# Where a two-layer network computes its modulation vectors: two of them leave the first mixer, and the second norm is modulated per channel

## Chip, cores and metric

One Trainium2 chip, one core of it. The metric is the device time of one execution in microseconds (us); the kernel before takes 2913.27 us (median of 3 runs, 2911.15 to 2913.72).

## What is computed

Two layers over 256 context and 512 latent tokens of width 1024, in fp32. Each layer takes six modulation vectors for the context and six for the latent tokens from `silu(c) @ w_ada[l] + b_ada[l]`. A vector pair (context, latent) is named (l, r) here, r = 0 to 5: shift, scale and gate of the mixer, then of the mixture of experts.

```python
for l in range(2):
    mod = split(silu(c) @ w_ada[l] + b_ada[l], 6)        # once for c, once for c_ctx
    h = rmsnorm(x, g_mix[l]) * (1 + mod[1]) + mod[0]
    x = x + mod[2] * (mixer_ab(h) if l == 0 else mixer_c(h))   # conv + pooling; mLSTM
    h = rmsnorm(x, g_ffn[l]) * (1 + mod[4]) + mod[3]
    x = x + mod[5] * moe(h)                               # 16 experts, top 2
out = rmsnorm(x_lat, g_final)
```

## The kernel before

All engines run one program written out by hand; each engine executes its instructions in that order, and semaphores join them. Most of the program is matrix work on TensorE (PE).

The stages in order of time: the start (norm of the input, modulation vectors (0, 0) and (0, 1)); the first mixer (value, gate and pool products on PE, a 31-tap convolution on VectorE (DVE), a pooling chain on GpSimd (POOL), then a layernorm over channels, whose sums are PE products with `onesd`, and the output projection); routing, and a scatter of the tokens into expert order by GpSimd's indirect DMAs; experts(0), a loop of 18 passes; the gap between experts(0) and the second mixer, in which chain(2) gathers the experts' rows, adds them to x, norms them and turns them to channels; the second mixer (product with `w_in_c`, in which every operand is split in a high and a low part and three fp32r products replace one fp32 product; gates; values; keys and queries; 16 attention units); its projection, routing, scatter and experts(1); the last norm.

**Modulation work.** `w_ada` is read in items. Eight items of 256 columns ("units", `n < UNITS`) give (0, 2) and (0, 3). From `n = UNITS` on, four items of 1 MB give one vector of `VECTORS`. `mods(n)` on PE waits for the item's load, and multiplies it with `scT` (two columns). The first item of a vector also adds the bias (`bada`). After the fourth, `vector_out(w)` on ScalarE (ACT) takes the 2 x 1024 result out of PSUM, and stores it in DRAM (`mods_d`), from where a chain loads it spread over 128 partitions (`load_mods`). Each fp32 product is two rows' worth of `x` in the trace (a count of 8 is four products). The table `ITEMS_AT` says after which step of the first mixer how many items have been done; sixteen items, vectors 0 to 3, stand there, and the other sixteen in the gap.

**chain(n)** norms tile t of 128 tokens: ACT takes the sum of squares and the root, DVE scales (`normed`), PE turns the tile to channels (`to_channels`), ACT copies it out of PSUM (`turned`). There is one pair of PSUM banks for the turned tile, so that tile t + 1 waits for `turned` of tile t. In chain(2) DVE also takes the low part from PSUM (`low_input`), and PE waits for that too.

**Pooling on PE** (`pooled` 6 and 7) waits for the last pooling step of GpSimd, and PE, which runs in order, has work behind that wait.

Of the kernel before, what the change touches and what calls it, by code (L numbers as in the profile page):

```python
# [51 lines left out]
NPAR = TAPS + 6  # L52
# [60 lines left out]
def program(nc, x, c, ctx_in, c_ctx, w_ada, b_ada, g_mix, g_ffn, g_final, w_in_ab, w_dw_a, b_dw_a, ln_g_a, ln_b_a,  # L113
# [13 lines left out]
    with es:  # L127
# [131 lines left out]
        MOD_OF = {0: (None, None), 1: ((0, 3), (0, 2)), 2: ((1, 0), (0, 5)), 3: ((1, 3), (1, 2)), 4: (None, (1, 5))}  # L259
        G_OF = {0: g_mix[0], 1: g_ffn[0], 2: g_mix[1], 3: g_ffn[1], 4: g_final}  # L260
        MODS = []
        for n in range(5):
            per = (2 if MOD_OF[n][0] else 0) + (1 if MOD_OF[n][1] else 0)
            MODS.append(MODS[-1] + 16 * (1 + per * (1 if n >= 3 else 2)) if n else 0)
# [22 lines left out]
        chl = [rounded(f"chl{i}", o, 2, 2048) for i, (o, n) in enumerate(CHUNKS[1:4])]  # L287
# [9 lines left out]
        def item_at(n):  # L297

            if n < UNITS:
                return at(26624 + 2048 * (n % 2), KD, UW)  # L300
            return at(26624 + 2048 * ((n - UNITS) % 3) if n < I_GAP else 14336 + 2048 * ((n - I_GAP) % 8), 2, D)

        def vector_ps(w):

            b = (0 if w % 2 == 0 else 3) if w < W_GAP else 2 * (w % 2)
# [8 lines left out]
        hTh, hTl = rounded("hTh", 0, KD, S), rounded("hTl", 44144, KD, S)  # L314
        craw = nc.alloc_sbuf_tensor_at("craw", [P, KD, 512], F32, offset=base + 4 * 30832)[:]
# [38 lines left out]
        def _(sp):  # L354
# [20 lines left out]
            for r, v in enumerate((b_dw_a, ln_g_a, ln_b_a, b_pool.rearrange("a g d -> a (g d)"), pool_scale, g_mix[0:1, :])):  # L375
# [17 lines left out]
            def load_mods(n):  # L393
# [12 lines left out]
                sp.dma_start(CH[n]["tmp"], G_OF[n].partition_broadcast(P)).then_inc(s_mod, 16)  # L406
# [17 lines left out]
            def chain(n):  # L424
# [5 lines left out]
                for i, (t, j) in enumerate(tiles):  # L430
# [9 lines left out]
                    if n == 2 and i < 4:  # L440
                        for m in (I_GAP + 8 + 2 * i, I_GAP + 9 + 2 * i):
                            sp.wait_ge(u_mm, m - 7 if i < 3 else I_GAP + 10)
                            item_load(m)
# [47 lines left out]
            sp.wait_ge(a_mm, 7)  # L491
# [26 lines left out]
            for i in range(2):  # L518
                sp.wait_ge(u_st[i], stored(W_GAP))
# [7 lines left out]
            for n in range(I_GAP, I_GAP + 8):  # L527
# [1493 lines left out]
```

## Time and profile before

| | |
|---|---|
| median of 3 runs | 2913.27 us |
| profiled execution, its own time | 2915.74 us |
| its span, first to last instruction | 2914.1 us |
| mean granted TensorE clock | 0.948 of 2.4 GHz |
| PE busy | 2665.9 us, 91% |
| DVE busy | 1838.9 us, 63% |
| ACT busy | 1295.8 us, 44% |
| POOL busy | 311.6 us, 11% |
| DMA | 675.38 MB, mean 232 GB/s |

The busy share is a mean over all stages. What an edit is worth is read at its place: which engine the others wait for there.

### The profile page before, as it was taken

What the parts mean: (1) busy time and instruction counts of PE and PEld (TensorE: products, weight loads), DVE (VectorE), ACT (ScalarE), POOL (GpSimd) and SP (SyncE); (2) the same over time, 40 slices, a digit from 0 to 9 for tenths busy, and PEclk for the clock granted to TensorE, in tenths of its full rate; (3) what the DMA queues carried; (4) which work ended last, traced back from release to release, by engine and by line L of the source; (5) the groups of instructions that cost most, each with busy time, mean ns of one, the idle gap of its engine ahead of it and who ended that gap; (6) DMA issues with size and microseconds to landing.
All of it is one profiled execution on the core that took longest, in us unless ns stands there. A gap on an engine that the chain in (4) does not pass through costs nothing.

```text
span 2914.1 us, 29092 instructions
## 1 busy us (share of the span) xinstructions
PE 2665.9 (91%) x10607; PEld 1839.7 (63%) x10607; DVE 1838.9 (63%) x1678; ACT 1295.8 (44%) x1201; POOL 311.6 (11%) x299
## 2 busy tenths in 40 slices
PE   8999989992999999999899997899795899999994
PEld 3555424452888888888268775555343788888883
DVE  4899813124888888888557312355322788888886
ACT  4000002012777777777221321355210677777773
POOL 0537540002000000000200020000001000000001
PEclk9999999995999999999999978999896899999997
DMA  8021174518999999997921311001406799999993
GB/s 305 29 72 56 34 269 181 197 70 326 372 388 385 391 388 384 382 389 297 374 76 58 114 36 55 0 26 37 159 36 260 300 383 387 385 386 389 385 380 129
DMA packets 157055, 675.38 MB, mean 232 GB/s; under 512 B 24745, under 2 KB 42233, under 8 KB 100544
## 3 DMA queue, kind: packets, MB, share of 16 engines
q1 hardware_dynamic: 134416, 595.27, 53.2%
q0 software_dynamic: 20208, 74.98, 6.8%
q10 hardware_dynamic: 2368, 4.28, 0.4%
q8 instruction: 41, 0.67, 0.1%
q14 instruction: 22, 0.18, 0.0%
HBM read 615.13 MB, written 59.35 MB: 231 GB/s over the span
## 4 chain that ended last, share of the span: by engine, by line
PE 87%; DMA 5%; DVE 4%; POOL 2%; ACT 2%; issue 1%; SPq 0%; POOLq 0%; DVEq 0%; ACTq 0%
PE ps L723 83%; PE ps L881 1%; ACT arena L1157 1%; PE ps L887 1%; DMA arena<-in_w_ada_dram 1%; DMA buf_d<-arena,slots 1%; POOL buf_d L650 1%; DMA arena<-buf_d,slots 1%; POOL arena L611 1%; DMA xs_d<-arena 0%; DMA chunk<-in_w_ada_dram 0%; PE ps L825 0%; DMA arena<-in_w_out_c_dram 0%; PE ps L1052 0%; DMA buf_d<-arena 0%
## 5 line engine op out<-in xcount | busy, mean ns | idle before, releaser
L1693 DVE TENSOR_TENSOR wl<-wx,wh 128x2048 fp32r<-128x2048 f32 x432 | 969.4, 2286 | 45.5 <-ACT wh L1157 45.5
L1157 ACT ACTIVATE wh<-wx 128x2048 fp32r<-128x2048 f32 x432 | 819.5, 1915 | 185.8 <-PE ps L723 147.6
L723 PE MATMUL ps<-arena 128*128 128x512 f32 (+3 forms) x2432 | 853.6, 511 | 47.8 <-DVE arena L1836 20.1
L723 PE MATMUL ps<-wh,xT 128*128 128x512 f32 x2304 | 736.7, 396 | 4.9 <-DVE xT L1710 4.9
L723 PEld LDWEIGHTS ps<-arena 128*128 128x128 f32 x2432 | 456.4, 200 | 430.2 <-issue 367.0
L723 PEld LDWEIGHTS ps<-wh,xT 128*128 128x128 f32 x2304 | 435.3, 189 | 105.9 <-DVE xT L1710 5.7
L723 PE MATMUL ps<-wl,xT 128*128 128x512 f32 x1152 | 455.4, 395 | 0.0
L1157 ACT ACTIVATE arena<-ps 128x512 f32<-128x512 f32 (+5 forms) x264 | 175.4, 682 | 519.7 <-PE ps L723 426.7
L723 PE MATMUL ps<-wh,gT 128*128 128x512 f32 x1152 | 378.1, 399 | 0.0
L1157 ACT ACTIVATE arena<-arena 128x1024 f32<-128x1024 f32 (+3 forms) x54 | 50.8, 945 | 453.9 <-DVE arena L1554 267.6
L723 PEld LDWEIGHTS ps<-wl,xT 128*128 128x128 f32 x1152 | 217.7, 189 | 47.3
L723 PEld LDWEIGHTS ps<-wh,gT 128*128 128x128 f32 x1152 | 216.8, 188 | 47.3
L1744 DVE SCALAR_TENSOR_TENSOR arena<-arena,par 128x768 f32<-128x768 f32 x232 | 241.0, 1114 | 0.0
L723 PE MATMUL ps<-wl,gT 128*128 128x512 f32 x576 | 226.0, 392 | 0.0
L723 PE MATMUL ps<-arena,scT 128*2 128x512 f32 (+1 forms) x384 | 143.7, 526 | 14.3 <-DMA arena<-in_w_ada_dram 14.3
L664 POOL DMA_DIRECT2D buf_d<-arena x36 | 19.4, 538 | 1230.7 <-ACT arena L1157 1230.7
L1553 DVE TENSOR_TENSOR arena<-ps,arena 128x1024 f32<-128x1024 f32 x10 | 12.2, 1225 | 209.0 <-PE ps L723 209.0
L723 PEld LDWEIGHTS ps<-wl,gT 128*128 128x128 f32 x576 | 108.3, 188 | 22.0
L881 PE MATMUL ps<-cst,arena 128*128 128x128 f32 x304 | 43.9, 289 | 76.9 <-DMA arena<-buf_d 76.9
L723 PEld LDWEIGHTS ps<-arena,scT 128*2 128x2 f32 x384 | 30.5, 85 | 118.0 <-issue 86.3
L1765 DVE TENSOR_TENSOR cwl<-craw,cwh 128x512 fp32r<-128x512 f32 (+1 forms) x48 | 39.9, 867 | 87.6 <-ACT cwh L1157 87.6
L881 PEld LDWEIGHTS ps<-cst,arena 128*128 128x128 f32 x304 | 43.2, 206 | 80.1 <-DMA arena<-buf_d 77.3
(229 smaller groups left out, 2208.5 us busy)
## 6 DMA issues: line engine op xcount, KB each, us to landing
wx<-in_w_dram SPq DMA_DIRECT2D x432, 1024.0 KB, 7.8
arena<-in_w_ada_dram SPq DMA_DIRECT2D x40, 1024.0 KB, 7.4
arena<-buf_d POOLq DMA_DIRECT2D x38, 512.0 KB, 10.3
buf_d<-arena POOLq DMA_DIRECT2D x36, 512.0 KB, 7.6
craw<-in_w_in_c_dram SPq DMA_DIRECT2D x8, 2048.0 KB, 8.7
buf_d<-arena POOLq DMA_DIRECT2D x1, 14848.0 KB, 47.3
arena<-in_w_in_ab_dram SPq DMA_DIRECT2D x8, 1024.0 KB, 10.3
arena<-in_w_out_ab_dram SPq DMA_DIRECT2D x4, 2048.0 KB, 10.4
```

The lines of the kernel that those rows point to most:

```text
L611: step(pool.tensor_copy(b[:, 0:CROWS - 1, PH + GRID_W:PW], b[:, 1:CROWS, PH:2 * PH]))
L650: pool.indirect_dma_start(buf_d, bass.IndirectOffsetOnAxis(ap=slots[:, k, t:t + 1], axis=0), hall[:, t, :], None).then_inc(s_scat, 16)
L664: pool.dma_start(buf_v[:, bass.ds(b + 1, 1), :].rearrange("p a d -> p (a d)"), yy).then_inc(m["yst"], 16)
L723: return pe.matmul(bank_ap, lhsT, rhs, start=first, stop=last)
L881: ins = pe.transpose(ps[:, 4 + k // 4, (k % 4) * P:(k % 4 + 1) * P], pairs(xg)[:, k // 2, k % 2, :], ident)
L887: ins = pe.transpose(ps[:, q, k * P:(k + 1) * P], pairs(gg)[:, 2 * q + k // 2, k % 2, :], ident)
L1157: return act.activation(out_, in_, f, **kw)
L1553: link(v.tensor_tensor(tmp, psf[:, b0:b0 + D], m[o + 2], ALU.mult))
L1693: v.tensor_tensor(wl[:, g], wx[:, g], whs[g % NH].bitcast(F32), ALU.subtract).then_inc(m["low"], 1)
L1744: ins = v.scalar_tensor_tensor(acc[k % 2], src, w, acc[k % 2], ALU.mult, ALU.add)
L1765: v.tensor_tensor(cwl[what], craw[what], cwh[what].bitcast(F32), ALU.subtract).then_inc(c_low, 1)
```

## The change

Of the ten vectors that follow the two of the start, six were computed in the first mixer and four in the gap. Now it is four in the first mixer (two by units, vectors 0 and 1), three in the gap (vectors 2, 3 and 4), and one each in three other stages: vector 5 one item behind each head of the values, vector 6 behind the last attention unit, vector 7 around the positions of the second routing.

Vectors 2 and 3, shift and scale of chain(2), are no longer stored and reloaded. PE turns them to channels, chain(2) only scales by the norm, and when all six tiles are turned, DVE (even) and ACT (odd) modulate the eight channel blocks, ACT rounds each to its high part and DVE subtracts for the low part; the first output block of the second mixer waits for them block by block. `load_mods(2)` issues two broadcast loads, where there were seven.

The values are taken out of PSUM by ACT alone (24 copies; 12 by ACT and 12 by DVE before), in front of its wait for DVE's scans for three of four heads. At the start, chunk 3 of `w_ada` (rows k = 5 and 6) is multiplied as fp32 and not split on ACT and DVE.

```diff
-        vstage = [at(1024 + D * (w % 2) if w < W_GAP else 13312, D) for w in range(W_ALL)]
+        vstage = [at(o, D) for o in (1024, 2048, 36976, 38000, 13312, 49520, 29696, 36976)]
...
-VECTORS = ((0, 4), (0, 5), (1, 0), (1, 1), (1, 2), (1, 3), (1, 4), (1, 5))
-W_GAP, W_ALL = 4, 8
+VECTORS = ((0, 4), (0, 5), (1, 0), (1, 1), (1, 3), (1, 2), (1, 4), (1, 5))
+ST_OF = [0, 1, None, None, 0, 1, 0, 1]
...
-ITEMS_AT = [0] * 9 + [*range(1, 9)] + [8 + 3 * i for i in range(1, 5)] + [I_GAP] * 2
+ITEMS_AT = [0] * 9 + [*range(1, 9)] + [10, 12, 14, 16, 16, 16]
@@ SP, first mixer
-            for n in range(UNITS, I_GAP):
+            for n in range(UNITS, 16):
                 sp.wait_ge(u_mm, max(n - 2, UNITS - 1 + min(n - UNITS, 1)))
                 item_load(n)
-                if n in (UNITS + 4, UNITS + 10):
-                    sp.wait_ge(ab_u, KD)
-                    out_panel(1, int(n > UNITS + 4))
-            sp.wait_ge(u_mm, I_GAP)
+            sp.wait_ge(ab_u, KD)
+            for q in range(2):
+                out_panel(1, q)
+            sp.wait_ge(u_mm, 16)
             for q in range(2):
                 out_panel(0, q)
@@ SP, after the second mixer's products
+            for n in range(28, 32):
+                if n == 31:
+                    sp.wait_ge(u_mm, 29)
+                item_load(n)
             sp.wait_ge(gr, R_A)
...
+            sp.wait_ge(u_mm, 32)
             sp.dma_start(abc.rearrange("p a b -> p (a b)"),
...
+                if u == 2:
+                    sp.wait_ge(kq_mm, KE)
+                    for n in range(32, 35):
+                        item_load(n)
...
+            sp.wait_ge(eE, 16)
+            item_load(35)
             sp.wait_ge(pV, 16)
...
+            for n in range(36, 40):
+                sp.wait_ge(u_mm, n - 3)
+                item_load(n)
             chain(3)
@@ PE, start
+            pe.wait_ge(up_in[3], 32)
+            whole(5, 3, 0)
+            turn_x0(4)
+            turn_x0(5)
+            whole(6, 3, 1)
@@ PE, to_channels
-                if n == 2 and t:
-                    pe.wait_ge(hl_rdy, t)
@@ PE, gap
-                if t < 4:
-                    mods(I_GAP + 8 + 2 * t)
-                    mods(I_GAP + 9 + 2 * t)
+                if t < 2:
+                    mods(24 + 2 * t)
+                    mods(25 + 2 * t)
+                if t == 2:
+                    pe.wait_ge(u_ev, UNITS + 4)
+                    for r in range(2):
+                        for k in range(KD):
+                            ins = pe.transpose(ps[:, 6, 16 * r + 2 * k:16 * r + 2 * k + 2],
+                                               vstage[2 + r][0:2, k * P:(k + 1) * P], ident[0:2, 0:2])
+                    ins.then_inc(a_mm, 1)
...
+                    if ct == 0:
+                        pe.wait_ge(hl_rdy, k + 1)
@@ PE, values, attention, projection
+                mods(28 + h)
+            pe.wait_ge(u_ev, UNITS + 6)
...
+            for n in range(32, 35):
+                mods(n)
             turn_y(15)
+            mods(35)
...
+            pe.wait_ge(u_ev, UNITS + 7)
...
+            for n in range(36, 39):
+                mods(n)
             positions(1)
+            mods(39)
+            pe.wait_ge(u_ev, UNITS + 8)
             experts(1)
@@ ACT, before the second mixer's first product
+            act.wait_ge(a_mm, 7)
+            high_slice(0)
+            act.wait_ge(md_v, 8)
+            for k in range(KD):
+                if k % 2:
+                    for v, cols in ((1, slice(0, S_CTX)), (0, slice(S_CTX, S))):
+                        ins = go(hTy[:, k, cols], hTx[:, k, cols], ACT.Identity, scale=mA[:, k, v:v + 1], bias=mB[:, k, v:v + 1])
+                    ins.then_inc(md_a, 1)
...
+                else:
+                    act.wait_ge(md_v, 9 + k // 2)
+                go(hTh[:, k, :], hTy[:, k, :], ACT.Copy).then_inc(md_a, 1)
@@ ACT, values
+            def v_out(h):
+                act.wait_ge(v_mm, h + 1)
+                for tt in range(NT):
+                    go(vv[h][:, tt, :], ps[:, tt, :], ACT.Copy).then_inc(v_ev, 1)
+            for h in range(3):
+                v_out(h)
             act.wait_ge(gr, R_X)
             go(r_fl[0:64, :], r_x[0:64, :], ACT.Exp, scale=-1.0).then_inc(ga, 1)
+            v_out(3)
+            vector_out(5)
@@ DVE, chain(2)
-            def low_input(t, j):
-                v.wait_ge(ht_rdy, j + 1)
-                cols = slice(t * P, (t + 1) * P)
-                v.tensor_tensor(hTl[:, :, cols], psf[:, 4 * 512:6 * 512].rearrange("p (k n) -> p k n", n=P),
-                                hTh[:, :, cols].bitcast(F32), ALU.subtract).then_inc(hl_rdy, 1)
...
+                    if nn == 2:
+                        v.tensor_scalar(dst, xt, rs[:, s:s + 1], None, ALU.mult).then_inc(h_rdy, 1)
```

How the order moves, at three places on PE. The first is the end of the first mixer's products. Rows with `arena,scT` are modulation products and `bada,cst` their bias; the other rows up to `onesd` are `pooled` 6 and 7, which wait for GpSimd. Before:

```order
L723 MATMUL ps<-arena,scT 2x512 x2
L723 MATMUL ps<-bada,cst 2x256 x4
L723 MATMUL ps<-arena,scT 2x512 x16
L723 MATMUL ps<-bada,cst 2x256 x4
L723 MATMUL ps<-arena,scT 2x512 x6
...
L723 MATMUL ps<-arena,scT 2x512 x10
L723 MATMUL ps<-bada,cst 2x256 x4
L723 MATMUL ps<-arena,scT 2x512 x14
...
L723 MATMUL ps<-arena,scT 2x512 x2
L723 MATMUL ps<-bada,cst 2x256 x4
L723 MATMUL ps<-arena,scT 2x512 x14
```

The same place now:

```order
L756 MATMUL ps<-arena,scT 2x512 x2
L756 MATMUL ps<-bada,cst 2x256 x4
L756 MATMUL ps<-arena,scT 2x512 x14
L756 MATMUL ps<-arena 128x512
L756 MATMUL ps<-arena 128x256
...
L756 MATMUL ps<-arena,scT 2x512 x2
L756 MATMUL ps<-bada,cst 2x256 x4
L756 MATMUL ps<-arena,scT 2x512 x14
```

One vector stands ahead of the wait for GpSimd and one between `pooled` 6 and 7, where one and a half stood ahead, one and a half between and one behind.

The second place is the gap: L825 (now L865) are the turned tiles of chain(2), and the row `hTh,cwh` is the second mixer's first product. Before, from the last item ahead of the first tile on:

```order
L723 MATMUL ps<-arena,scT 2x512 x14
L825 MATMUL ps<-cst,arena 128x128 x8
L723 MATMUL ps<-arena,scT 2x512 x2
L723 MATMUL ps<-bada,cst 2x256 x4
L723 MATMUL ps<-arena,scT 2x512 x6
L825 MATMUL ps<-cst,arena 128x128 x8
L723 MATMUL ps<-arena,scT 2x512 x8
L825 MATMUL ps<-cst,arena 128x128 x8
L723 MATMUL ps<-arena,scT 2x512 x2
L723 MATMUL ps<-bada,cst 2x256 x4
L723 MATMUL ps<-arena,scT 2x512 x6
L825 MATMUL ps<-cst,arena 128x128 x8
```

The same place now:

```order
L756 MATMUL ps<-arena,scT 2x512 x14
L865 MATMUL ps<-cst,arena 128x128 x8
L756 MATMUL ps<-arena,scT 2x512 x2
L756 MATMUL ps<-bada,cst 2x256 x4
L756 MATMUL ps<-arena,scT 2x512 x6
L865 MATMUL ps<-cst,arena 128x128 x8
L756 MATMUL ps<-arena,scT 2x512 x8
L865 MATMUL ps<-cst,arena 128x128 x8
L1059 MATMUL ps<-cst,arena 128x2 x16
L865 MATMUL ps<-cst,arena 128x128 x24
L756 MATMUL ps<-hTh,cwh 128x512
```

The vector that stood between tiles 2 and 5 is gone, and 16 small transposes of vectors 2 and 3 stand there.

The third place is the second routing: `wrt` are the router's products, `cst` and `ones` with 16 to 64 columns the positions. Now:

```order
L756 MATMUL ps<-wrt,arena 128x16 x8
L756 MATMUL ps<-arena,scT 2x512 x2
L756 MATMUL ps<-bada,cst 2x256 x4
L756 MATMUL ps<-arena,scT 2x512 x10
L756 MATMUL ps<-arena,cst 128x16
L756 MATMUL ps<-arena,cst 128x48
```

Before, the row with `cst 128x16` followed directly on `wrt`.

## Rows read from the trace of the kernel before

**Rows 1.** The page: chain that ended last, share of the span by engine

```profile
PE 87%; DMA 5%; DVE 4%; POOL 2%; ACT 2%; issue 1%; SPq 0%; POOLq 0%; DVEq 0%; ACTq 0%
```

**Rows 2.** Timeline of PE, start: start, us, engine, line, operation, [idle before <-releaser]

```profile
48.20 5.29 PE L723 MATMUL ps<-chunk,scT 128*2 128x512 f32 x8
```

**Rows 3.** Chain that ended last: start, first projection, second mixer: start us, us, what

```profile
38.23 5.70 PE ps L723 x24
...
468.79 55.20 PE ps L723 x128
...
1477.02 136.97 PE ps L723 x768
```

**Rows 4.** Timeline of PE, end of the first mixer's products

```profile
394.96 5.46 PE L723 MATMUL ps<-arena 128*128 128x512 f32 x8 [4.71 <-POOL arena L635]
...
424.94 2.85 PE L723 MATMUL ps<-arena 128*128 128x512 f32 x8
427.72 1.88 PE L723 MATMUL ps<-arena,scT 128*2 128x512 f32 x4
...
431.34 12.18 PE L723 MATMUL ps<-arena,scT 128*2 128x512 f32 x28
444.67 0.67 PE L723 MATMUL ps<-arena,onesd 128*128 128x512 f32 x1 [1.15 <-issue]
```

**Rows 5.** Windows: us, busy of PE, PEld, DVE, ACT, POOL, PEclk, DMA share, GB/s

```profile
690.00:700.00 10.00, 0.00 (x0) 0.00 (x0) 0.00 (x0) 0.00 (x0) 4.05 (x5) 0.50 1.03 420
...
1477.00:1483.00 6.00, 5.98 (x19) 5.11 (x20) 3.37 (x3) 1.36 (x2) 0.00 (x0) 0.50 0.24 59
```

**Rows 6.** Chain that ended last, the scatter's end

```profile
694.31 12.97 DMA buf_d<-arena,slots
```

**Rows 7.** Timeline of PE, gap between experts(0) and second mixer

```profile
1430.53 3.57 PE L723 MATMUL ps<-arena,scT 128*2 128x512 f32 x4 [9.34 <-DMA arena<-in_w_ada_dram]
...
1449.64 1.09 PE L825 MATMUL ps<-cst,arena 128*128 128x128 f32 x8
...
1472.15 1.37 PE L825 MATMUL ps<-cst,arena 128*128 128x128 f32 x8 [2.46 <-DVE hTl L1532]
1477.02 0.79 PE L723 MATMUL ps<-hTh,cwh 128*128 128x512 f32 x1 [3.50 <-DVE cwl L1765]
```

**Rows 8.** Timelines of ACT (modulation at the start, high parts), of DVE (low parts)

```profile
56.27 4.89 ACT L1157 ACTIVATE arena<-arena,mB,mA 128x256 f32<-128x256 f32 x8 [1.73 <-DVE mB L1519]
...
1474.48 3.88 ACT L1157 ACTIVATE cwh<-craw 128x1024 fp32r<-128x1024 f32 x4
...
1475.75 4.62 DVE L1765 TENSOR_TENSOR cwl<-craw,cwh 128x1024 fp32r<-128x1024 f32 x4
```

**Rows 9.** Timeline of PE, values to keys

```profile
1793.03 5.62 PE L723 MATMUL ps<-arena 128*128 128x128 f32 x48 [1.18 <-DVE arena L1804]
1814.80 8.53 PE L723 MATMUL ps<-arena 128*128 128x128 f32 x48 [16.14 <-DVE arena L1836]
...
1840.81 36.32 PE L723 MATMUL ps<-arena 128*128 128x256 f32 x96 [1.62 <-DVE st L1839]
```

**Rows 10.** Timeline of ACT, first values

```profile
1813.02 1.54 ACT L1157 ACTIVATE arena<-ps 128x512 f32<-128x512 f32 x3
```

**Rows 11.** Timeline of PE, last attention unit, projection

```profile
2072.15 7.69 PE L723 MATMUL ps<-arena 128*128 128x512 f32 x12
2085.00 1.12 PE L1124 MATMUL ps<-cst,arena 128*128 128x128 f32 x4 [5.15 <-DVE arena L1892]
2093.19 32.37 PE L723 MATMUL ps<-arena 128*128 128x512 f32 x70 [7.08 <-DMA arena<-in_w_out_c_dram]
```

**Rows 12.** Timeline of PE, second routing

```profile
2220.62 3.59 PE L723 MATMUL ps<-wrt,arena 128*128 128x16 f32 x16 [1.11 <-ACT arena L1157]
2229.34 1.09 PE L723 MATMUL ps<-arena,cst 128*128 128x16 f32 x4 [5.12 <-DVE arena L1631]
2230.23 1.93 PE L723 MATMUL ps<-arena,ones 128*128 128x16 f32 x8
```

More of the change, by code:

```diff
@@ L439, in chain @@
                         sp.dma_start(craw, wc[:, :, 0:512]).then_inc(cw, 16)
[L440 to L443, printed above, removed]
+                    if n == 2 and i < 2:
+                        sp.wait_ge(u_mm, 18 + 2 * i)
+                        item_load(24 + 2 * i)
+                        item_load(25 + 2 * i)
                     if i + ahead < len(tiles):
@@ L526, in _ @@
             nb = experts(0)
-            for n in range(I_GAP, I_GAP + 8):
-                sp.wait_ge(moe[0]["used"], nb * PAIRS + max(n - I_GAP + 4 - 7, 0))
+            for n in range(16, 24):
+                sp.wait_ge(moe[0]["used"], nb * PAIRS + max(n - 16 + 4 - 7, 0))
                 item_load(n)
@@ L576, in _ @@
             expert_weights(1, 0, None, range(8))
-            chain_start(4)
+            await_stores(sp, 4)
+            for t, j in tiles_of(4)[:2]:
+                load_x(4, t, j)
             sp.wait_ge(lg_rdy, lg_before(3, NT))
             expert_weights(1, 0, None, range(8, PAIRS))
+            sp.wait_ge(u_st[1], stored(8, 1))
+            load_mods(4)
             experts(1)
@@ L765, in _ @@
             pe.wait_ge(up_in[0], 32)
-            whole(0, 0)
+            whole(0, 0, 0)
             for r in range(8):
                 bias(psf[0:2, UW * r:UW * r + UW], r)
-            for i in range(3):
+            for i in range(2):
                 early(2 * i + 1)
@@ L1006, in _ @@
             experts(0)
-            for n in range(I_GAP, I_GAP + 8):
+            for n in range(16, 24):
                 mods(n)
@@ L1292, in _ @@
                 act.wait_ge(up_in[i + 1], 32)
-                for o in range(2):
+                for o in range(2 if i < 2 else 0):
                     if i:
@@ L1498, in _ @@
             for i in range(3):
-                for o in range(2):
+                for o in range(2 if i < 2 else 0):
                     v.wait_ge(a_hi, 2 * i + o + 1)
@@ L1768, in low_slice, with modulated @@
                 low(ct, (slice(None), slice(None), slice(ct % 4 * P, ct % 4 * P + P)))
-            for ct in range(4):
+            v.wait_ge(a_mm, 7)
+            v.scalar_tensor_tensor(mA[:], ps[:, 6, 2 * KD:4 * KD].rearrange("p (k v) -> p k v", v=2), 1.0,
+                                   bc(par[:, :, TAPS + 6], 2, 2), ALU.add, ALU.mult).then_inc(md_v, 1)
+            v.tensor_copy(mB[:].rearrange("p k v -> p (k v)"), ps[:, 6, 0:2 * KD]).then_inc(md_v, 1)
+            low_slice(0)
+            v.wait_ge(md_v, 8)
+            v.wait_ge(ht_rdy, 3 * NT)
+            def modulated(k):
+                for i, cols in ((1, slice(0, S_CTX)), (0, slice(S_CTX, S))):
+                    ins = v.tensor_scalar(hTy[:, k, cols], hTx[:, k, cols], mA[:, k, i:i + 1], mB[:, k, i:i + 1],
+                                          ALU.mult, ALU.add)
+                ins.then_inc(md_v, 1)
+            modulated(0)
+            for k in range(KD):
+                if k % 2 == 0 and k + 2 < KD:
+                    modulated(k + 2)
+                v.wait_ge(md_a, 4 + (k + 1) + (k + 1) // 2)
+                v.tensor_tensor(hTl[:, k, :], hTy[:, k, :], hTh[:, k, :].bitcast(F32), ALU.subtract).then_inc(hl_rdy, 1)
+            for ct in range(1, 4):
                 low_slice(ct)
@@ L1938, in arrived, with stored @@
     return 16 * sum(1 for i in range(I_LAST[n] + 1) if I_SEM[i] == I_SEM[n])
-def stored(w, i=0):
-    return 16 * (UNITS // 2 + (w + 1 - i) // 2)
+def stored(w, i):
+    return 16 * (UNITS // 2 + sum(1 for m in range(w) if ST_OF[m] == i))
 def pairs(a):
```

117 lines of the change are left out of this document (64 added, 53 removed).

## The prediction

> **What bounds the kernel now.** I read the page first: 87% of the chain that ended last is PE [rows 1]. PE executes in program order, so each product in front of a stage delays it unless PE would have waited there. I therefore followed the chain in time, and read PE's timeline at each place that the diff touches: who ends PE's wait, and what stands on PE behind it. Two kinds of places come out. In the first mixer PE waits for GpSimd until 394.96 and has 2.5 vectors to do after that, so these lengthen the kernel by their full time. In the gap PE waits for a load (9.34 us before 1430.53) and then works through three more items between the turned tiles. Elsewhere PE idles for DVE's scans (16.14 us before 1814.80), for a load before the projection (7.08 us), and for the second routing's DVE chain (5.12 us) [rows 4, 7, 9, 11, 12].
>
> **Price of a vector.** The last one of the first mixer runs from 427.72 to 431.34 + 12.18 = 443.5: 15.8 us, of which an item is 8 of 32 instructions, 3.45 us, and the bias 1.9 us [rows 4]. The total stays the same; only places move.
>
> **1. Start.** Two k of chunk 3 cost PE 5.70 us as split products [rows 3]. The fp32 form took 5.29 us for one k in 48.20, right after an idle spell; warm it is an item of two k less one, 8 instructions, 3.45 us [rows 2, 4], so 6.9 us for two. PE gains nothing, but both highs on ACT and lows on DVE leave, the second k fills PE's wait for the last turned tile, and chunk 4's k then starts warm. I take -2 us, bounds 0 and -3.
>
> **2. First mixer.** GpSimd's end is not touched, so PE resumes at 394.96. Then: `pooled` 6, 5.46 us (half clock, the same work takes 2.85 later); vector 1, 15.8 + 0.5; `pooled` 7, 2.85 [rows 4]. The layernorm's sums start at 419.6 + 0.4 = 420.0 and not 444.67: -24.6 us. What could be late next is the output projection's weights: 4 MB now queue behind item 15 at about 406 and 4 MB at 416.7. At the 420 GB/s of a full queue [rows 5] all of it has landed by 430, and the projection, which stood 24.1 us behind the sums' start (468.79 [rows 3]), starts at 444. Item 15's load needs item 12 done (406) and is wanted at 413; a 1 MB transfer takes 2.4 us of a free queue. Bounds: -27, and -20 if that load and the weights are late.
>
> **3. First scatter.** `load_mods(2)` issues seven broadcasts of 0.5 MB just ahead of the scatter; five go, 2.5 MB. The queue is full then, DMA share 1.03 at 420 GB/s [rows 5], and the last scatter, issued at 694.31, lands 12.97 us later [rows 6]. 2.5 MB are 6.0 us of such a queue. The landing can't go below what a scatter takes by itself, for which the nearest row is half of that 12.97. I take -5, bounds 0 (if the queue's head, not its length, delays it) and -6.5.
>
> **4. Gap.** PE's first two vectors and tile 0 stay, and so does the wait for the next items' load to 1430.53, since the same 2 MB of `w_in_c` and two items stand ahead of it. PE reaches tile 2 at 1449.64 as before [rows 7]. There vector 4's second half and the fourth one used to follow; now two rows of 8 small transposes (1 to 2.2 us by a tile's 1.09, beside ACT's copy) and tiles 3, 4, 5, each 1.09 us on PE and 1.0 on ACT in turn (its 1024-column copy is 0.97 [rows 8]), 2.2 us a tile. The last tile is copied at 1459.9. Then, on the path: high part of weight slice 0, 3.88 / 4 = 0.97; its low part, 4.62 / 4 = 1.15; modulation of block 0, at most 4.89 / 4 = 1.22; then ACT's loop over eight blocks, each a copy of 0.85 (768 of 1024 columns; between 0.73 and 0.97), four with a modulation of 1.22 and a wait of 0.1 besides: 12.1 us; a subtraction of 0.96 (0.9 to 1.15 by the low part's) and PE's last block, 1.05 [rows 8]. PE ends output block 0 at 1459.9 + 3.3 + 12.1 + 2.0 = 1477.3. Before, it started block 0 at 1477.02; the 16 blocks took 136.97 us with 6 us at half clock, so a block is 8.4 us, and the first ended 8.4 + 3 after its start, at 1488.4 [rows 3, 5, 7]. Gain: 11 us. Bounds: -14 (ACT's loop shorter, less DMA work), -5 (a tile's rows come late: six tiles' gathers and x loads share the queue, and DVE's additions wait for them).
> On the modulation: the Trainium skill, VectorE: DVE Perf Modes (section on the TRN2 errata), says that operands from SBUF pay a fixed extra time per instruction, so that small tiles are dear, which speaks against 256- and 512-column pieces. Its table gives, as an estimate, 0.40 + 0.61 us for such a pair on ScalarE where the row gives 1.22; by the page the gap would gain 0.9 us more, by the row, which decides here, it is as above.
>
> **5. Values.** Before, the second head's products wait until DVE's scans end: 14.80 follows 1793.03 + 5.62 by 16.14 us, then runs cold at 8.53. Now ACT evicts at 0.51 us a copy [rows 10], 3.1 us a head, less than the item (3.45; 5.3 with bias) that PE does meanwhile. PE runs 4 x 5.62 + 3 x 3.45 + 5.3 = 38.1 us without a gap, to 1831.2; then ACT's copy of the vector 1.0, the small transposes and their copies 1.5; keys start at 1833.8 and not 1840.81 [rows 9]: -7 us. Behind SP's new wait for item 31 stands only the load of `abc`, issued at 1831 and first read after the keys, 1877 [rows 9]; ACT's and GpSimd's attention work waits for it. Bounds -8, -4.
>
> **6. Last unit.** The last unit's products end at 2079.8; PE then idled, did the last turned block and waited for `w_out_c` until 2093.19 [rows 11]. Now three items with bias 12.2, that block 1.1, item 35 3.45, ACT 1.05: projection at 2079.8 + 18.1, 4.7 us later, but with PE warm, which I price at -2. +3 us, bounds +1 and +6. This is the place where cover is too short: 17 us of new work in 13 us of wait.
>
> **7. Second routing.** Items 36 to 38 stand between the router's last product (2224.2) and the positions, which DVE's chain waits for. PE is at half clock there: 16 products of 16 columns in 3.59 us [rows 12]. Cold for 3 more us (half of the 6 seen at 1477 [rows 5]), the items take 12.2 + 1.5 to 3, until 2238.5; the positions then run warm, 1.5 for 2.8, and DVE resumes at 2240.5 and not 2232.3: +8. Later weights have drained from the queue when the scatter comes, -1. +7 us, bounds +4 and +18.
>
> **Sum.** -2 - 24.6 - 5 - 11 - 7 + 3 + 7 = -39.6 us. Made against the profiled execution's own 2915.7 it gives 2876.1; the median of the runs is 2.5 lower, so 2873.6, rounded to **2874**.
>
> **Rivals.**
> A, late transfers in the first mixer (chance 0.12): weights or item 15 hold PE, half of term 2 is lost. For: PE does wait for items in the old trace, in the gap 9.34 us [rows 7]. Against: the queue has room by 430. Time 2886.
> B, half clock through the routing (0.10): if PE does not come up to 2.4 GHz inside items 36 to 38, 24 instructions and the bias take 24 us and the positions 2.8, DVE resumes at 2251 and term 7 is +17. For: the clock reads low all along there. Against: in 1477 to 1483 PE, busy without a break, has 0.50, and then comes up. Time 2884.
> The Trainium skill, TensorE: Matmul & The Clock Gate (What's actually happening), has the array at half rate by default and lets go only under sustained activity. By that rule items 36 to 38, which stand back to back, are themselves what lifts it, as in my term 7; with interrupted work it would be rival B.
> C, the gap gains nothing (0.07): gathers set the end, the modulation is added behind them; time 2884.
> D, slower (0.04), one mechanism: PE is idle 15 us and not 4.71 before 394.96 and stays at 1.2 GHz through the layernorm and the projection. Each us so spent costs 0.5, so it must last more than 79 us to eat 39.6; the 24.1 us of the sums and the first 55.20 us of the projection [rows 3] together would just do it, and twice that would give 2874 + 79 = 2953. Against: after the 4.71 us the half clock held only for about 6 [rows 4].
>
> **How the numbers follow.** The forecast has 0.67, with its own range 2866 to 2882 from the bounds of the terms, which don't fall on one side together. Rivals A to C reach 2886; two of them together, 2896. The range 2861 to 2889 leaves out D, joint rivals, and sums near the lower bounds. A measurement of this kernel tells 0.2%, 5.8 us. Faster by more than that: all but D and 0.01 of mishaps together, 0.95; same 0.01; slower 0.04.
>
> **What would show it.** PE's sums with `onesd` start about 26 us earlier (terms 1 and 2); the last scatter lands about 8 us after its issue; the first product of `hTh` and `cwh` comes some 12 us earlier relative to the loop's end but trickles in over 12 us; no idle of PE between the heads of the values, keys 7 us sooner after the gates; projection 18 us after the last unit; positions 16 us after the router's last product. Wrong would be: PE waiting for `w_out_ab` or item 15, DVE waiting for gathered rows after 1440, or a half clock beyond 10 us in any stage that is PE's.

## The result, and the profile after

The changed kernel takes 2868.08 us (median of 4 runs, 2864.67 to 2871.49) against 2913.49 us of the kernel before (2911.15 to 2916.94). The ratio is 0.9843, 95% interval 0.9824 to 0.9862: 1.6% faster, clear of the spread of the runs, and inside the predicted range of 2861 to 2889.

The profiled execution took 2864.67 us, its span is 2863.1 us, the mean granted clock 0.957. From the page of the profile, the busy time of each engine, and below it the shares of the chain that ended last (they answer to [rows 1]):

```profile
PE 2655.8 (93%) x10615; PEld 1833.5 (64%) x10615; DVE 1819.0 (64%) x1668; ACT 1308.6 (46%) x1227; POOL 310.7 (11%) x299
...
PE 89%; DMA 3%; DVE 3%; POOL 2%; ACT 2%; issue 1%; SPq 0%; ACTq 0%; POOLq 0%; DVEq 0%
```

PE is busy for 10 us less (its half-clock stretches differ too); 51.0 us left the span. So most of what was gained is waiting, and it has to be looked for place by place. The chain that ended last gives the stations (start, us, what); the table behind it sets the time between stations beside that of before:

```profile
440.15 55.20 PE ps L756 x128
...
665.67 5.53 DMA buf_d<-arena,slots
...
675.41 1.99 PE ps L921 x8
...
1746.22 38.31 PE ps L756 x232
1786.88 34.64 PE ps L756 x96
...
2040.51 55.17 PE ps L756 x128
...
2165.86 18.84 PE ps L756 x60
```

| stretch (from, to) | before us | after us | difference | predicted |
|---|---|---|---|---|
| span's start, first product of the first mixer | 57.29 | 56.02 | -1.3 | -2 |
| to PE's resumption behind GpSimd | 337.67 | 336.50 | -1.2 | 0 |
| to the output projection | 73.83 | 47.63 | -26.2 | -24.6 |
| to experts(0)'s first turn | 242.69 | 235.26 | -7.4 | -5 |
| to the loop's last stretch on the chain | 667.62 | 666.79 | -0.8 | 0 |
| to the z products of the second mixer (the gap lies in it) | 240.57 | 231.06 | -9.5 | -11 |
| to the values | 173.36 | 172.96 | -0.4 | 0 |
| to the keys | 47.78 | 40.66 | -7.1 | -7 |
| to the attention | 37.28 | 35.59 | -1.7 | 0 |
| to the projection's second stretch on the chain | 273.32 | 274.16 | +0.8 | +3 |
| to the router's last product | 69.21 | 69.23 | 0 | 0 |
| to experts(1)'s first turn | 44.94 | 48.50 | +3.6 | +7 |
| to the end | 648.54 | 648.74 | +0.2 | 0 |
| sum | 2914.1 | 2863.1 | -51.0 | -39.6 |

The timeline of PE at the end of the first mixer's products answers to [rows 4]:

```profile
392.52 5.25 PE L756 MATMUL ps<-arena 128*128 128x512 f32 x8 [14.67 <-POOL arena L667]
397.69 1.88 PE L756 MATMUL ps<-arena,scT 128*2 128x512 f32 x4
399.50 1.89 PE L756 MATMUL ps<-bada,cst 48*2 48x256 f32 x8
401.32 12.18 PE L756 MATMUL ps<-arena,scT 128*2 128x512 f32 x28
413.42 2.85 PE L756 MATMUL ps<-arena 128*128 128x512 f32 x8
416.11 10.48 PE L756 MATMUL ps<-arena,onesd 128*128 128x512 f32 x32
```

PE now idles 14.67 us before GpSimd's end, and has one vector behind it. The sums (`onesd`) start 23.6 us after PE resumes; before they started 49.7 us after. In the gap (it answers to [rows 7]):

```profile
1394.02 3.57 PE L756 MATMUL ps<-arena,scT 128*2 128x512 f32 x4 [9.72 <-DMA arena<-in_w_ada_dram]
...
1413.59 1.15 PE L1059 MATMUL ps<-cst,arena 2*128 2x2 f32 x16
1414.87 1.06 PE L865 MATMUL ps<-cst,arena 128*128 128x128 f32 x8
1418.84 1.97 PE L865 MATMUL ps<-cst,arena 128*128 128x128 f32 x8 [2.91 <-DVE arena L1649]
1422.01 1.94 PE L865 MATMUL ps<-cst,arena 128*128 128x128 f32 x8 [1.21 <-ACT hTx L1216]
1430.07 0.76 PE L756 MATMUL ps<-hTh,cwh 128*128 128x512 f32 x1 [6.12 <-DVE hTl L1861]
```

The load still ends PE's first wait. New is the wait of 2.91 us before the fifth tile, for DVE's norm. That norm stands in DVE's program behind the additions of the sixth tile, and DVE waits before the additions of the fifth and the sixth (5.36 and 1.25 us), by the profile for their x, which is loaded back (`arena<-xs_d`):

```profile
1406.06 0.75 DVE L1633 TENSOR_SCALAR arena<-arena,wsel 128x1024 f32<-128x1024 f32 x1 [5.36 <-DMA arena<-xs_d]
```

Values and second routing (they answer to [rows 9, 12]):

```profile
1757.21 5.62 PE L756 MATMUL ps<-arena 128*128 128x128 f32 x48
...
2165.86 3.59 PE L756 MATMUL ps<-wrt,arena 128*128 128x16 f32 x16 [1.11 <-ACT arena L1216]
2169.38 3.33 PE L756 MATMUL ps<-arena,scT 128*2 128x512 f32 x4
2172.64 1.89 PE L756 MATMUL ps<-bada,cst 48*2 48x256 f32 x8
2174.46 8.75 PE L756 MATMUL ps<-arena,scT 128*2 128x512 f32 x20
2183.13 0.65 PE L756 MATMUL ps<-arena,cst 128*128 128x16 f32 x4
```

The second head of the values follows without a wait and at full clock, and the positions stand 13.7 us behind the end of the router's last product, where they stood 5.1 us.

### The profile page after: what moved, and what is told of

The parts are those of the page before. It is cut to its first block, busy times and chain, and to the rows that moved or that the text cites. A ratio compares the mean times of both kernels' runs of the same rounds, so it can differ in the third digit from the quotient of the medians.

```text
span 2863.1 us, 29115 instructions
## 1 busy us (share of the span) xinstructions
PE 2655.8 (93%) x10615; PEld 1833.5 (64%) x10615; DVE 1819.0 (64%) x1668; ACT 1308.6 (46%) x1227; POOL 310.7 (11%) x299
## 4 chain that ended last, share of the span: by engine, by line
PE 89%; DMA 3%; DVE 3%; POOL 2%; ACT 2%; issue 1%; SPq 0%; ACTq 0%; POOLq 0%; DVEq 0%
PE ps L756 85%; PE ps L921 1%; PE ps L927 1%; ACT arena L1216 1%; POOL buf_d L682 1%; DMA arena<-buf_d,slots 1%; DMA arena<-in_w_ada_dram 1%; POOL arena L643 1%; PE ps L865 1%; DMA chunk<-in_w_ada_dram 0%; DMA buf_d<-arena,slots 0%; PE ps L1101 0%; DMA buf_d<-arena 0%; PE ps L1187 0%; POOL arena L652 0%
## 5 line engine op out<-in xcount | busy, mean ns | idle before, releaser
L756 PE MATMUL ps<-arena 128*128 128x512 f32 (+3 forms) x2432 | 843.5, 506 | 31.0 <-POOL arena L667 14.7
L756 PEld LDWEIGHTS ps<-arena 128*128 128x128 f32 x2432 | 450.6, 197 | 411.9 <-issue 369.2
L756 PE MATMUL ps<-hTh,cwh 128*128 128x512 f32 (+1 forms) x256 | 88.1, 344 | 6.5 <-DVE hTl L1861 6.5
```

The costliest lines, as they stand in the source:

```text
L756: return pe.matmul(bank_ap, lhsT, rhs, start=first, stop=last)
```

## The experiments

All start from the changed kernel. The ratios are to runs of the kernel before that were made beside them: 2914.61 us for half, gitems, gcraw and vsplit, 2914.41 for same, bothahead, route and bcast, 2914.19 for routelate, gapcraw and gapthree.

**same.** No edit.

> The changed kernel once more, nothing edited. It should take 2868 us again; two levels about 7 us apart (2864.7 and 2871.5) were seen in its four runs, and a profile of a run at the upper level would show in which stage those 7 us stand.

It took 2867.05 us (4 runs: 2868.23, 2865.11, 2874.55, 2865.87), ratio 0.9842 (0.9822 to 0.9861). Two levels are not borne out: 2868.23 lies between them. None of the traces is of a long execution, but the longest of the four has the lowest mean granted clock: 0.956, 0.956, 0.953 and 0.956 in the same order. If PE was at 1.2 and not 2.4 GHz for longer by so much that the mean falls by 0.003, that is 8.6 us of 2870, about what the third run is longer (an estimate). The trace of its first run lies 3.2 us behind that of the result at experts(1)'s first turn; 2.2 us of it stand between the second mixer's first product and the values, 1.7 us in the keys and queries (36.33 for 34.64 us). So the traced execution of the result was a short one. Single executions of this kernel spread over 9.4 us, and a difference of a few us between two kernels' times says little by itself; below I use the stretch in the trace that an edit touches.

**bothahead and half.** Both vectors, or one and a half, ahead of the wait for GpSimd.

```diff
-ITEMS_AT = [0] * 9 + [*range(1, 9)] + [10, 12, 14, 16, 16, 16]
+ITEMS_AT = [0] * 9 + [*range(1, 9)] + [12, 16, 16, 16, 16, 16]   # bothahead
+ITEMS_AT = [0] * 9 + [*range(1, 9)] + [11, 14, 14, 16, 16, 16]   # half
```

> The changed kernel with both vectors 0 and 1 ahead of the wait for GpSimd (ITEMS_AT ends 12, 16, 16, 16, 16, 16). The theory of term 2, that only work behind that wait lengthens the kernel, says: vector 1's 15.8 us fill the 14.67 us of idle and run over by 1.2; pooled 6 follows warm, 2.9 for 5.25 us; the projection starts 15 us sooner, at 425, and the kernel takes 2853. The rival, that the projection's weights then set its start (8 MB, the last 4 of them issued at 393.7), gives at most half of that, 2860.

> The changed kernel with two more items (half of vector 1, with its bias, 8.8 us) ahead of the wait for GpSimd. All of it fits into the 14.67 us of idle: PE resumes at 392.5 as now, has 7 us of items left behind it, and the projection starts 8.8 us sooner, at about 431. If the items ahead did delay GpSimd or the loads, the gain would be smaller.

bothahead took 2854.14 us (2853.7 to 2857.07), ratio 0.9795 (0.9779 to 0.9811); half, one run, 2863.72. PE's timeline of bothahead has the output projection at 424.00, 16.15 us before that of the result (425 and 2853 us were expected); the rival of late weights fell. half has it at 432.50, 7.65 us sooner (431 was expected), and shows where 1.7 us of its 8.8 went, in the second sums of the layernorm:

```profile
392.97 4.21 PE L756 MATMUL ps<-arena 128*128 128x512 f32 x8 [5.71 <-POOL arena L667]
397.12 7.03 PE L756 MATMUL ps<-arena,scT 128*2 128x512 f32 x16
...
406.76 10.48 PE L756 MATMUL ps<-arena,onesd 128*128 128x512 f32 x32
419.17 12.28 PE L756 MATMUL ps<-arena,onesd 128*128 128x512 f32 x32 [1.92 <-ACT arena L1216]
```

The idle falls from 14.67 to 5.71 us by the 8.8 us put there, GpSimd's end stays within 0.5 us, and what stands behind the wait is paid in full: term 2's mechanism. The same 32 products took 10.59 us in the result. And half lost another 5.0 us in the gap: its items there ran at half clock for longer (3.57, 3.57 and 7.94 us for 3.57, 1.89 and 5.31), and the second mixer's first product came 83.24 us after the gap's first item, not 78.24.

**bcast.** The five broadcast loads come back; nothing reads them. The modulation rows of (0, 3) stand in for those that are no longer stored.

```diff
-        MOD_OF = {0: (None, None), 1: ((0, 3), (0, 2)), 2: (None, (0, 5)), 3: ((1, 3), (1, 2)), 4: (None, (1, 5))}
+        MOD_OF = {0: (None, None), 1: ((0, 3), (0, 2)), 2: ((0, 3), (0, 5)), 3: ((1, 3), (1, 2)), 4: (None, (1, 5))}
...
-                if n != 2:
+                if n:
                     sp.dma_start(CH[n]["tmp"], G_OF[n].partition_broadcast(P)).then_inc(s_mod, 16)
@@ ACT
             experts(0)
+            act.wait_ge(s_mod, MODS[2])
             vector_out(2)
```

> The changed kernel with the five broadcast loads of 0.5 MB put back into load_mods(2); nothing reads them. Term 3 says that 2.5 MB ahead of the scatter in a full queue delay its landing by 5 to 7 us: the last scatter lands 12 to 13 us after its issue and not 5.5, and the kernel takes 2874. The rival, that the scatter only waits for the head of the queue, gives 2868 to 2869.

It took 2879.15 us (2877.51 to 2881.51), ratio 0.9876 (0.986 to 0.9893), 12.1 us over same. The chain that ended last, around the first scatter:

```profile
665.63 13.55 DMA buf_d<-arena,slots
...
679.46 3.86 DMA arena<-buf_d
...
683.37 2.00 PE ps L921 x8
```

The last scatter is issued at the same moment as in the result (665.67) and lands 8.0 us later, and experts(0) starts 8.0 us later: the theory holds, the rival falls, and the price is more than I gave it (13.55 us for 12 to 13, and 2879 for 2874). In the twelve traces that have no such loads, the result's among them, this landing took 5.3 to 6.6 us, so 8.0 is at the upper end of 6.9 to 8.3. The bytes say where it comes from. From 650 us to the landing GpSimd's queue (q0, the scatters) moves 6.29 MB in both traces, SP's (q1) 4.60 MB here and 1.93 in the result: 2.67 MB more, 6.4 us at 420 GB/s. Of the stretch 656 to 662 the view of the DMAs (queue: packets, MB, share) has

```profile
q1 hardware_dynamic: 345, 1.27, 51.8%
q0 software_dynamic: 339, 1.26, 51.1%
```

so the two queues share evenly while both have work, and SP's extra bytes are through before the scatters, of which there are more, have ended. About 0.6 us more is a dip of the DMA engines from 652 to 654 us (0.78 busy, 1.02 in the result); the rest is within the spread of the landing.

What the time has beyond 8.0 us does not stand at the broadcasts: against the result's trace 3.0 us more lie in the gap and 2.5 us, net, in the second routing, where the same items ran at half clock for longer. All four runs are long, and whether the later start of these stages brings it or chance isn't shown.

**vsplit.** The values' copies divided again, ACT's behind the wait for the scans.

```diff
             def v_out(h):
                 act.wait_ge(v_mm, h + 1)
-                for tt in range(NT):
+                for tt in range(0, NT, 2):
...
-            for h in range(3):
-                v_out(h)
             act.wait_ge(gr, R_X)
             go(r_fl[0:64, :], r_x[0:64, :], ACT.Exp, scale=-1.0).then_inc(ga, 1)
-            v_out(3)
+            for h in range(4):
+                v_out(h)
@@ DVE, behind R_M
+            for h in range(H):
+                v.wait_ge(v_mm, h + 1)
+                for tt in range(1, NT, 2):
+                    v.tensor_copy(vv[h][:, tt, :], ps[:, tt, :]).then_inc(v_ev, 1)
```

> The changed kernel with the values taken out of PSUM by ACT and DVE as before the change, items 28 to 31 left between the heads. Term 5 says that the second head then waits for DVE's scans again: PE idles 12 us before it, the keys start 7 to 12 us later and the kernel takes 2876. Rival: the item between the heads covers most of the wait, and it costs under 3 us.

It took 2884.10 us (2882.98 to 2886.95), ratio 0.9897 (0.988 to 0.9913). PE's timeline, second head:

```profile
1771.64 8.57 PE L756 MATMUL ps<-arena 128*128 128x128 f32 x48 [10.70 <-DVE arena L1927]
```

10.70 us of idle and 2.95 us of half clock (8.57 for 5.62) are 13.65, and the keys do start 13.65 us later relative to the values. The theory holds and the rival falls; the price is above the 7 to 12 us that I expected, and the time above 2876. Of the rest of the difference (17 us to same) 2.3 us stand in the second routing, again at half clock: the scatter is issued 4.2 us later and lands 1.9 us faster. The clean reading of the edit is 13.65 us. It undoes two things at once, ACT as the only engine that copies and its place ahead of the wait for the scans, and does not say what each is worth.

**route and routelate.** All of vector 7 behind the positions; then also load_mods(4) behind experts(1)'s weights.

```diff
@@ PE, both
-            for n in range(36, 39):
-                mods(n)
             positions(1)
-            mods(39)
+            for n in range(36, 40):
+                mods(n)
@@ SP, routelate alone
-            sp.wait_ge(u_st[1], stored(8, 1))
-            load_mods(4)
             experts(1)
+            sp.wait_ge(u_st[1], stored(8, 1))
+            load_mods(4)
```

> The changed kernel with all four items of vector 7 behind the positions of the second routing, where PE idles 26 us. If the items cost what DVE waits for them, the positions start about 7.6 us sooner but run at half clock (3.0 for 1.7 us), so the last scatter is issued 6 us sooner and the kernel takes 2862. The rival: the items' loads, landed long before, only hid a wait for the scatter's queue, and the gain is under 2 us.

> The run route (vector 7's items behind the positions) with load_mods(4) also moved: its two broadcast loads of 0.5 MB are issued behind experts(1)'s last weights and not just ahead of experts(1). In route the scatter was issued 8.2 us sooner, but 4.0 us were given back, of which the first gather took 6.54 for 3.78 us beside these loads. Theory: that gather takes 3.8 us again and experts(1) starts 2.7 us sooner than in route (2862). Rival: the gather was slow for another reason, and nothing changes against route (2865).

route took 2865.04 us (2864.11 to 2865.59), ratio 0.9829 (0.9812 to 0.9845): 2.0 us under same, which by the times alone is no difference (2862 was expected, and under 2 us of gain by the rival; the trace decides for the theory). routelate took 2859.67 us (2858.17 to 2865.26), ratio 0.9824 (0.9805 to 0.9843) to 2914.19 us. From the router's last product to the issue of the last scatter the traces have 37.94 us in the result, 29.74 in both of these (before 30.68): the items cost 8.2 us there. To experts(1)'s first turn it is 48.50, 44.29 and 42.77. The chain of route and of routelate, in that order:

```profile
2200.50 7.36 DMA buf_d<-arena,slots
...
2208.45 6.54 DMA arena<-buf_d
```

```profile
2195.67 8.54 DMA buf_d<-arena,slots
...
2204.81 3.85 DMA arena<-buf_d
```

Issued 8.2 us sooner, the scatters meet the tail of 4 MB of weights that are issued with the router's last product: in the result the DMA engines' busy share falls to 0.22 (2192.86 to 2195.86) as the eight scatters begin at 2193.99; in routelate, where they begin at 2186.78, it is 1.01 through all of them. The last scatter takes 7.36 or 8.54 us where it took 6.13; and in route the gather shares the engines with the two broadcast loads. In route 1.2 of the 8.2 us go back at the scatter and 2.8 at the gather, in routelate 2.4 and 0.1. The gather's 3.85 us in routelate shows that the loads had slowed it; the net gain of moving them is 1.5 us and not the 2.7 expected, since the scatter took 1.2 us longer, which may be chance.

**gitems, gcraw, gapcraw, gapthree.** The gap's transfers. gitems: loads of items 24 to 27 sooner. gcraw: the load of `w_in_c` with tile 2. gapcraw: gitems, and `w_in_c` with tile 3. gapthree: gapcraw, and a third pair of buffers for gathered rows.

```diff
@@ SP, gitems, gapcraw, gapthree: in front of chain(2), not in it
+            for n in range(24, 28):
+                sp.wait_ge(u_mm, 18 + 2 * (n // 26))
+                item_load(n)
             chain(2)
@@ SP, gcraw (gapcraw and gapthree: i == 3)
-                    if n == 2 and i == 0:
+                    if n == 2 and i == 2:
                         sp.dma_start(craw, wc[:, :, 0:512]).then_inc(cw, 16)
@@ POOL, gapthree, chain(2) alone
+                    if n == 2:
+                        s, ys, ready = i % 3, y_sets, (*y_in, s_fill)[i % 3]
+                        if i == 2:
+                            pool.wait_ge(u_mm, 21)
+                        if i > 2:
+                            pool.wait_ge(x_new, j - 2 - NT)
...
```

> The changed kernel with the loads of items 24 to 27 issued right behind those of items 16 to 23, and not behind chain(2)'s first stores and the 2 MB of w_in_c. The queue is idle from about 1370 to 1377 and full from 1377 to 1405. Theory: PE's wait of 9.72 us before 1394.02 goes, the x loads of the later tiles land sooner, and the gap is 3 to 6 us shorter (2864). Rival: the gathered rows share the engines with the items, tile 0 comes later, and nothing is gained or 2 us lost.

> The changed kernel with the 2 MB load of w_in_c issued with chain(2)'s tile 2 and not tile 0; it is first read at 1424.9. Theory: items 24 to 27 and the x loads land about 5 us sooner, and the gap ends 3 to 5 us sooner. Rival: the load then lands late for ACT's high part, at 1410 to 1415 at best, and the gap is as long as now.

> Both edits of the gap in one: items 24 to 27 loaded behind items 16 to 23, and the 2 MB of w_in_c issued with tile 3. If the stores and x loads of the tiles, slowed by these 6 MB, set when tiles 4 and 5 come, the fifth tile is turned at 1412 and not 1418.8 and the gap is 6 us shorter. If the gathers of tile 4 and 5 set it, each of which waits until two tiles before are added, the gain stays at 2 us, as in gitems.

> The run gapcraw with a third pair of buffers for the gathered rows in chain(2), so that each gather waits for the tile three before it and not two. In gitems the last tile's rows were issued at 1402.14, when tile 3 had been added, and landed 10 us later. Theory: that wait sets the gap's end; with the third pair the second mixer starts 6 to 10 us sooner than in the changed kernel, 2859 to 2861. Rival: the turned tiles then wait for the x loads instead, and it is as gapcraw.

Times: gitems 2866.90 us (2865.55 to 2869.64), ratio 0.9842 (0.9826 to 0.9858); gcraw 2866.88 (2864.7 to 2874.32), 0.9845 (0.9824 to 0.9866); gapcraw, one run, 2861.95; gapthree 2862.93 (2859.39 to 2867.27), 0.9834 (0.9816 to 0.9852). From the first item to the second mixer's first product the traces have 78.24 us in the result, 76.48, 76.77, 76.96 and 69.81 in these four. PE's timeline of gitems:

```profile
1386.05 1.88 PE L755 MATMUL ps<-arena,scT 128*2 128x512 f32 x4
...
1402.95 1.09 PE L864 MATMUL ps<-cst,arena 128*128 128x128 f32 x8
...
1408.51 1.97 PE L864 MATMUL ps<-cst,arena 128*128 128x128 f32 x8 [3.39 <-DVE arena L1648]
1417.90 1.97 PE L864 MATMUL ps<-cst,arena 128*128 128x128 f32 x8 [7.42 <-DVE arena L1648]
```

PE's wait of 9.72 us is gone and the third tile is turned at 1402.95, not 1412.57, but the fifth comes at 1417.90, not 1418.84: the time became a wait for DVE. GpSimd's timeline of gitems and DVE's say what DVE waits for:

```profile
1402.14 1.74 POOL L705 DMA_INDIRECT arena<-buf_d,slots  x1 [5.17 <-DVE arena L1635]
```

```profile
1412.39 0.75 DVE L1632 TENSOR_SCALAR arena<-arena,wsel 128x1024 f32<-128x1024 f32 x1 [3.94 <-DMA arena<-buf_d,slots]
```

The last gather is issued only when DVE has added tile 3, two tiles before (tiles count from 0, so this gather is the sixth's), and its rows arrive 10 us after. In gapcraw the last wait of DVE is of like length, but the profile puts it down to the x load of that tile, issued 2.6 us behind the gather:

```profile
1409.53 0.75 DVE L1632 TENSOR_SCALAR arena<-arena,wsel 128x1024 f32<-128x1024 f32 x1 [4.48 <-DMA arena<-xs_d]
```

With a third pair of buffers, laid where item 20 was (gapthree), the last gather goes out at 1390.20, the fifth tile is turned at 1410.53, and 8.4 us of the gap are gone, 7.2 of them against gapcraw. So of the forecasts: the 3 to 6 us of gitems and the 3 to 5 of gcraw were 1.8 and 1.5; moving both loads (gapcraw) gave 1.3 and not the 6 of its first theory; the buffers gave 7.2, as expected. That the wait for a free buffer held the gap up is shown; whether the sixth tile's rows or its x then come last differs from trace to trace, since both go through the same DMA engines. By the times gapthree is 4 us under same, which the spread would hide, and 2 above its forecast; the low time of gapcraw is one run, whose trace has 2.5 us of it at the start.

**best.** bothahead, routelate and gapthree in one.

> The edits of bothahead, routelate and gapthree in one kernel. They touch three stages that lie far apart on PE's path, so their gains should add: against the unedited changed kernel (2867 in the run same) -16 us before the first projection by the traces, -8.4 in the gap, -5.7 to -7 from the router's last product to experts(1). That gives 2836 to 2838, ratio 0.974 to the kernel before. The rival: PE, idle at other moments, works longer at half clock elsewhere (3 to 5 us of such differences were seen between traces), and 2843 is reached at best.

It took 2839.94 us (5 runs, 2833.95 to 2841.9) against 2911.96, ratio 0.9749 (0.9735 to 0.9762). That is 2 to 4 us above the forecast and 3 below the rival's. In its trace (span 2832.3 us, clock 0.961) the first mixer is 16.1 us shorter than in the result (17.0 less 0.9 by which vector 1 overruns GpSimd's end), the gap 6.7 for an expected 8.4, and the stretch from the router's last product to experts(1) 7.0. The gains add but for some 2 us in the gap. It beats the changed kernel by 27 to 28 us.

## Why the prediction was right, point by point

**Sum.** -39.6 us were predicted, the pair of profiled executions has -51.0, the medians -45.4. Of the 5.6 us between the last two, 3.4 are a short traced execution of the changed kernel (2864.67 for a median of 2868.08) and 2.2 a long one of the kernel before (2915.74 for 2913.49). Part of what the traces have beyond the terms is luck of the clock: the keys and queries ran in 34.64 us where 36.33 was seen before and in most of the other traces. That is the -1.7 in the row to the attention, and no term had it. More than half of the gain is the first mixer.

**Terms 1 and 2** held: -1.3 for -2, and -26.2 for -24.6. Most of the 1.6 us over are waits of 0.5 and 0.4 us that I added and that did not come. GpSimd's end moved by 2.4 us, not by 0: 1.3 of them is the start, the other 1.2 us stand in the first mixer's first 442 products, 142.75 us for 143.92. They begin at half clock in both; the windows have 0.50 from 60 to 63 us before and 0.92 from 59 to 62 after, so the clock rose sooner. No experiment separates this, nor term 1. half and bothahead show the mechanism from the other side.

**Term 3, the scatter,** is a mis-sized term: -5 predicted with a bound of -6.5, -7.4 found, and +8.0 when the loads came back. The step that failed is that the landing would not go below half of 12.97 us; it went to 5.53 (5.3 to 6.6 over the traces). The 2.5 MB cost what their bytes take (2.67 MB more in SP's queue, 6.4 us) and something more, of which 0.6 us is placed. The scatter goes by GpSimd's queue and the broadcasts by SP's. The Trainium skill, DMA: Bandwidth & Descriptors (Queues, rings and completion order), says that the engines take turns between queues, packet by packet. The trace of bcast agrees: 1.26 MB of the one and 1.27 MB of the other from 656 to 662 us. Turns do not spare the scatter these bytes, since it has 6.29 MB to move itself and the broadcasts are through first.

**Term 4, the gap,** came out at -9.5 for -11, and its working held in most places: first tile and load as before, last tile copied 2 us later than predicted (at 1425.0; reckoned from the loop's end, 1423.0 was predicted), ACT's loop 11.3 us for 12.1. The two late microseconds are the bound that I named, rows that come late. What I did not see is that this wait lay just under PE's work, and that a third pair of buffers and two moved loads would give another 8.4 us. gitems shows that making PE sooner is worth little there: it took 9.7 us of PE's wait away for 1.8 us. half shows the other side: PE's items took 4.3 us longer and its first load ended 0.9 us later against the gap's first item, and the gap grew by 5.0. Two chains, PE's and DVE's, end close together. No experiment separates the vector that left the gap from the modulation per channel: term 4 has them as one sum.

**Term 5, the values,** held: -7.1 for -7. PE ran 38.31 us for a predicted 38.1. vsplit prices the covered wait at 13.65 us; the item behind each head fills part of what it saves.

**Term 6, the last unit,** was +0.8 for +3. From the start of the last unit's products the projection came 23.98 us later, before 21.04: 2.9 us, where I had 4.7. Of the 1.8 us between, 1.3 is that these products ran warm (6.42 for 7.69 us), which no step foresaw: luck of the clock. The pieces that I named add up to 17.8 us and not the 18.1 of the text; 17.6 were found. No experiment covers this term. The projection's own first stretch on the chain took 2.1 us less, as priced at 2.

**Term 7, the second routing,** was +3.6 for +7. The issue of the last scatter moved by +7.3, predicted +8; the 3.7 us given back by a drained queue, predicted 1, were mis-sized. route confirms both: the items cost 8.2 us there, and 4.0 come back. In the ten traces that have the items in this order the landing took 4.2 to 6.1 us, so this term moves by some 2 us with the execution.

**Rivals.** A: no wait for `w_out_ab` was seen, not even in bothahead, where the projection starts 16 us sooner. C, the gap gains nothing: not in the time, but in part in the mechanism. DVE does wait late in the gap, 5.36 us before 1406.06 (reckoned from the loop's end, 1443 in the kernel before), where I had named a wait for gathered rows after 1440 as a sign of being wrong. It is for x rows by the trace, and the last tile comes 2 us late. D: after 14.67 us of idle the half clock lasted 5.2 us. B, half clock through the routing, happened in part, in other executions: bcast's timeline has

```profile
2184.27 3.57 PE L756 MATMUL ps<-arena,scT 128*2 128x512 f32 x4
2187.77 3.57 PE L756 MATMUL ps<-bada,cst 48*2 48x256 f32 x8
2191.27 11.19 PE L756 MATMUL ps<-arena,scT 128*2 128x512 f32 x20
```

against 3.33, 1.89 and 8.75 in the result: 4.4 us more up to the scatter's issue, 1.9 of them given back by a shorter landing. I had priced it at 10 us, with the clock down through all of the items; here it rose inside the last row.

## What to carry to other kernels

Work on an in-order engine is priced by its side of the nearest wait: 8.8 us moved to the near side of GpSimd's wait brought the layernorm's sums 9.8 us closer to GpSimd's end (half), while 9.7 us of idle removed in the gap were worth 1.8, since another engine's chain ended last there (gitems). So ask of each freed stretch what is the next to be late, and look for buffers that let a gather or load go only when the tile two before is done. A transfer that nothing waits for still costs: 2.5 MB ahead of a scatter were 8.0 us, and 1 MB of loads beside a gather made it 2.7 us longer, of which 1.5 us were left in the net.

## What the runs showed of the hardware

The moment at which PE's clock rises under unbroken work varies from run to run of the same instructions. The windows of the result and of bcast over the same items of the gap, then of the second routing (start:end, us, busy of PE, PEld, DVE, ACT, POOL, PEclk, DMA share, GB/s):

```profile
1394.00:1398.00 4.00, 3.98 (x7) 0.55 (x8) 2.69 (x3) 0.00 (x0) 0.00 (x0) 0.56 1.02 420
1398.00:1404.50 6.50, 6.50 (x19) 1.30 (x17) 2.62 (x4) 0.00 (x0) 2.33 (x2) 1.00 1.03 413
...
2166.00:2172.50 6.50, 6.50 (x20) 3.68 (x20) 2.55 (x8) 1.33 (x2) 0.00 (x0) 0.51 1.01 426
2172.50:2183.00 10.50, 10.50 (x29) 2.19 (x28) 2.62 (x13) 0.00 (x0) 0.00 (x0) 1.00 1.02 422
```

```profile
1401.80:1410.00 8.20, 8.16 (x14) 1.39 (x15) 5.32 (x6) 0.00 (x0) 1.78 (x2) 0.50 1.03 417
2184.30:2195.00 10.70, 10.70 (x18) 1.75 (x18) 5.17 (x20) 0.22 (x1) 0.00 (x0) 0.50 1.01 425
```

In the result PE comes up from 1.2 GHz (0.50) to 2.4 GHz (1.00) within 4 us of the gap's items and some 3 us of the routing's; in bcast it is at 1.2 GHz for over 8 and over 10 us, with PE busy throughout. The Trainium skill, TensorE: Matmul & The Clock Gate (What's actually happening), says that activity releases the throttle and that the moment of release differs between runs of one kernel; the traces agree, with 3 to over 10 us here, a wider spread than the page has. At one such place it is worth up to 5 us (half, in the gap). With several such places in the program it is the likely reason why the runs of one kernel spread over 2865 to 2875 us; their mean clock says so, and no trace of a long run is there to show it.

Two queues that both have work share the DMA engines evenly by bytes (1.26 and 1.27 MB in 6 us of bcast), and a scatter's end waits for all that the other queue moves until then.
